# A two-layer hybrid kernel: rewritten S5 mixer (array halves, tree, straight steps) and two MoE result arrays in place of three

## The reference, cut to what matters

```python
u = grp(h); y = u * d                     # the skip with d, by channel
for di, rev in enumerate((False, True)):
    # lam_bar, b_bar from a, log_step, b
    _, h_ctx = s5_scan(u_c, lam_bar, b_bar, c_mat, h0, rev, False)    # context first
    yl_d, _ = s5_scan(u, lam_bar, b_bar, c_mat, h_ctx, rev, True)     # then the latents
    y = y + yl_d
z = gelu(y); val, gt = split(z @ glu_w + glu_b, 2)
return val * sigmoid(gt)
```

## Time and profile before

| | us |
|---|---|
| median of 3 runs | 2813.92 (2813.19 to 2816.01) |
| profiled execution, device time | 2811.32 |
| its span in the trace | 2809.6 |
| prepare | 0 to about 218 |
| mixer 0 | to 658 |
| MoE of layer 0 (route, loop, combine) | 658 to 1610 |
| S5 mixer | 1610 to 2022 |
| MoE of layer 1 | 2022 to 2809.6 |

### The profile page before, as it was taken

How to read it: one execution, slowest core, us unless ns; L and a number is a source line. 1 busy time by engine, 2 the same in 40 slices (tenths; PEclk the granted TensorE clock), 3 DMA queues, 4 the chain that set the end, 5 groups by cost and what they waited for, 6 DMA issues and landing times. The chain is left out here.

```text
span 2809.6 us, 41115 instructions
## 1 busy us (share of the span) xinstructions
PE 2204.6 (78%) x12118; PEld 1269.5 (45%) x12119; DVE 972.7 (35%) x2063; ACT 612.7 (22%) x1083; POOL 582.3 (21%) x470
## 2 busy tenths in 40 slices
PE   3877998995969999999998046099786999988882
PEld 2774544743434444444444045084343444444441
DVE  4963365933322112121121447832232111111113
ACT  2342423612112112121121031031121221211110
POOL 2750000001022222222222304000002222233332
PEclk9998999997979999999999566559897999999996
DMA  9973102005089999999997546042129999999994
GB/s 322 411 309 121 60 30 75 1 1 221 31 329 364 356 354 365 348 365 352 353 370 234 212 115 175 0 151 78 70 114 363 364 364 357 340 363 390 391 381 153
DMA packets 178229, 685.01 MB, mean 244 GB/s; under 512 B 34298, under 2 KB 37818, under 8 KB 133370
## 3 DMA queue, kind: packets, MB, share of 16 engines
q1 hardware_dynamic: 129642, 581.86, 53.5%
q0 software_dynamic: 38848, 71.14, 10.6%
q10 hardware_dynamic: 9648, 30.81, 2.7%
HBM read 628.15 MB, written 95.63 MB: 258 GB/s over the span
## 5 line engine op out<-in xcount | busy, mean ns | idle before, releaser
L1424 PE MATMUL pGUw_m<-wguw_m,xTw_m 128*128 128x512 f32 x800 | 357.8, 600 | 22.3 <-issue 21.9
L1435 PE MATMUL pGUn_m<-wgun_m,xTn_m 128*64 128x256 f32 x2816 | 323.3, 382 | 30.0 <-issue 20.5
L1435 PEld LDWEIGHTS pGUn_m<-wgun_m,xTn_m 128*64 128x64 f32 x2816 | 208.8, 137 | 175.9 <-issue 82.3
L1424 PEld LDWEIGHTS pGUw_m<-wguw_m,xTw_m 128*128 128x128 f32 x800 | 148.5, 191 | 232.8 <-issue 232.8
L1474 PE MATMUL pYn_m<-wdn_m,hidTn_m 128*64 128x512 f32 x704 | 189.9, 615 | 18.1 <-DVE hidTn_m L1379 16.3
L1453 PE MATMUL pYw_m<-wdw_m,hidTw_m 128*128 128x512 f32 x400 | 191.8, 602 | 15.5 <-DVE hidTw_m L1365 15.5
L1228 POOL DMA_INDIRECT xgw_m<-moe_h,idxw_m x58 | 60.5, 1043 | 650.4 <-PE pTw_m L1410 618.0
L1234 POOL DMA_INDIRECT xgn_m<-moe_h,idxn_m x96 | 101.4, 1056 | 250.8 <-DVE idxn_m L1355 212.4
L872 POOL MEMSET zero_r<- 128x1024 f32 x2 | 1.9, 952 | 713.2 <-POOLq L69 443.6
L1255 POOL DMA_INDIRECT moe_acc<-yn_m,idxn_m x88 | 141.4, 1607 | 27.5 <-issue 27.5
L1362 DVE TENSOR_TENSOR hidw_m<-hsilw_m,pGUw_m 128x256 f32<-128x256 f32 x50 | 21.1, 421 | 326.7 <-ACT hsilw_m L1297 326.7
(11 more groups left out here) (378 smaller groups left out, 3406.2 us busy)
## 6 DMA issues: line engine op xcount, KB each, us to landing
wgun_m<-in_exp_w_gate SPq DMA_DIRECT2D x88, 1024.0 KB, 9.9
wgun_m<-in_exp_w_up SPq DMA_DIRECT2D x88, 1024.0 KB, 15.7
wdn_m<-in_exp_w_down SPq DMA_DIRECT2D x88, 1024.0 KB, 15.8
wguw_m<-in_exp_w_gate SPq DMA_DIRECT2D x50, 1024.0 KB
wguw_m<-in_exp_w_up SPq DMA_DIRECT2D x50, 1024.0 KB
wdw_m<-in_exp_w_down SPq DMA_DIRECT2D x50, 1024.0 KB, 12.7
w_p<-in_mod_w SPq DMA_DIRECT2D x24, 2048.0 KB, 16.5
acc_c<-moe_acc SPq DMA_DIRECT2D x30, 512.0 KB, 11.3
```

The source lines that it names most:

```text
L1424: last = pe.matmul(pGU_w[:], xT_w[b % 2][:, k, :], wgu[0][b % WIDE_RING][:, :, k, :], start=(k == 0), stop=(k == KD - 1))
L1435: last = pe.matmul(pGU_n[H * side:H * side + H, b % 2], xT_n[b % 2][:, k % 4, H * (k // 4):H * (k // 4) + H], w[:, :, k, P * side:P * side ...
```

## The change

**MoE.** Array 2 is gone. Route zeroes one array on ACT's queue in place of two. All narrow adds go to array 1, and POOL waits before each that the narrow add before it has landed. Combine loads two arrays; POOL's sum is gone.

**Prepare.** The skip d is put into the table of the within-chunk matmuls: `Dd` is loaded (512 KB), multiplied by the identity on DVE, and added to the K tables by four 16x16 matmuls for each half batch. UD, the Z sum and their waits are gone from S5.

**S5 front.** X comes in four DMAs, the squares of a quarter wait only for it, and Tb's loads on POOL wait for all four. DVE squares lam four times (powers for the tree) ahead of the norm.

**Recurrence.** The 32 context chunks are folded by a tree of five levels, four operations each; the latents' 63 steps are written out one after another, with no loop.

**After it.** The Tb and from_states matmuls exchange their operands: 64 columns of U or SV are stationary, 128 columns of Tb or Wb move, and two groups lie in the two column halves of the array. The sum lies in PSUM with chunks as rows, gelu reads it there, and `turn`, 16 small matmuls by the identity for each batch, gives what the GLU needs. SP issues the first half of the GLU weights once all copies of states are done, ahead of the Wb loads of batches 6 and 7.

```diff
@@ moe_route @@
-            for acc in accs[1:]:
-                for t in range(NT):
-                    act.dma_start(acc[t * P:(t + 1) * P, :], zero[:]).then_inc(zero_out, 16)
+            for t in range(NT):
+                act.dma_start(accs[1][t * P:(t + 1) * P, :], zero[:]).then_inc(zero_out, 16)
@@ moe_loop @@
                 pool.wait_ge(N['y_done'], i + 2)
+                pool.wait_ge(yn_added[(b + 1) % 2], q * (16 * UNROLL // 2) + 16 * ((b + 1) // 2) + 16)
                 pool.sem_inc(N['pool_go'], 1)
-                pool.indirect_dma_start(acc_half[1 + b % 2], bass.IndirectOffsetOnAxis(idx[1][b][:].bitcast(U32), 0),
+                pool.indirect_dma_start(acc_half, bass.IndirectOffsetOnAxis(idx[1][b][:].bitcast(U32), 0),
@@ moe_combine @@
-        @block.gpsimd
-        def _(pool):
-            for t in range(NT):
-                pool.wait_ge(acc_in[t], 48)
-                pool.tensor_tensor(acc1[:, t, :], acc1[:, t, :], acc2[:, t, :], ALU.add).then_inc(half_sum, 1)
-
...
-                dve.wait_ge(acc_in[t], 48)
-                dve.wait_ge(half_sum, t + 1)
+                dve.wait_ge(acc_in[t], 32)
@@ prepare @@
+            sp.dma_start(Dd[:].rearrange("p g i -> p (g i)"), io['s5_d'].to_broadcast([P, SG * SI])).then_inc(S['d_in'], 16)
...
+            dve.tensor_tensor(Dd[:], Dd[:], ident[:, 0:SI].rearrange("p (o i) -> p o i", o=1).to_broadcast([P, SG, SI]),
+                              ALU.mult).then_inc(S['dd_done'], 1)
...
+                            for g in range(4):
+                                pe.matmul(pK[32 * g:32 * g + SI, 7 * SI:8 * SI], ident[:, 0:SI], Dd[:, n * GB + 4 * half + g, :],
+                                          start=False, stop=False, skip_group_check=True)
@@ s5_mixer, SP @@
-            sp.dma_start(X[:], xin.rearrange("(c t) d -> c t d", t=SL)).then_inc(S['x_in'], 16)
+            for j in range(4):
+                sp.dma_start(X[:, 2 * j:2 * j + 2, :], xin.rearrange("(c t) d -> c t d", t=SL)[:, 2 * j:2 * j + 2, :])\
+                  .then_inc(x_in[j], 16)
...
+                if b == 5:
+                    sp.wait_ge(S['t_mm'], NB)
+                    sp.wait_ge(S['sf_done'], NB)
+                    sp.wait_ge(S['sb_done'], NB)
+                    glu_half(0)
...
+            glu_half(1)
@@ s5_mixer, POOL @@
+            for j in range(4):
+                pool.wait_ge(x_in[j], 16)
...
-            pool.tensor_tensor(UD, U[:, :, 0:NCL], vcol[:, 5].rearrange("p (g o) -> p g o", o=1).to_broadcast([P, SG, NCL]),
-                               ALU.mult).then_inc(S['ud_done'], 1)
@@ s5_mixer, ACT @@
+            for b in range(3):
+                states(b)
             for b in range(NB):
...
+                gelu(b)
+                if b % 2 == 0 and b >= 2:
+                    turned(b - 1)
+                if b + 3 < NB:
+                    states(b + 3)
+            turned(NB - 1)
@@ s5_mixer, DVE @@
+            dve.wait_ge(S['l8_in'], 16)
+            for level in range(4):
+                re, im = lam[:, level, 0], lam[:, level, 1]
+                done(dve.tensor_tensor(sqr[:, 0], re, re, ALU.mult))
+                done(dve.tensor_tensor(sqr[:, 1], im, im, ALU.mult))
+                done(dve.scalar_tensor_tensor(out=lam[:, level + 1, 1], in0=re, scalar=2.0, in1=im, op0=ALU.mult, op1=ALU.mult))
+                done.wait()
+                done(dve.tensor_tensor(lam[:, level + 1, 0], sqr[:, 0], sqr[:, 1], ALU.subtract))
+                done.wait()
...
-            with dve.Fori(0, 47) as q:
...
+            for level in range(5):
+                n, step = 16 >> level, 2 << level
+                early = VH[:, step // 2 - 1:NCC:step].rearrange("p n a g -> p n (a g)")
+                late = VH[:, step - 1:NCC:step]
...
+            for q in range(STEPS):
+                prev, here = VH[:, NCC - 1 + q], VH[:, NCC + q]
...
-                dve.tensor_tensor(Z[:, b * GB:(b + 1) * GB, :], ps[:, b * 512:(b + 1) * 512].rearrange("p (g c) -> p g c", g=GB),
-                                  UD[:, b * GB:(b + 1) * GB, :], ALU.add).then_inc(S['zs_done'], 1)
@@ s5_mixer, PE @@
+            def out_of(b, h, q):
+                return ps[64 * h:64 * h + 64, b * 512 + q * P:b * 512 + (q + 1) * P]
...
+                            last = pe.matmul(out_of(b, h, q), SV[:, part, b * GB + g, :],
+                                             Wb[b % 2][:, part, g, 0:SL, :].rearrange("p k i -> p (k i)"),
+                                             start=False, stop=(part == 1), skip_group_check=True)
...
+            def turn(b):
+                pe.wait_ge(S['z_done'], b + 1)
...
+                        last = pe.matmul(ps[at, b * 512 + t * NCL:b * 512 + (t + 1) * NCL], rows[at, t], ident[at, at],
+                                         start=True, stop=True, skip_group_check=True)
+                last.then_inc(S['zT_mm'], 1)
+
+            from_states(0)
+            for b in range(1, NB):
+                from_states(b)
+                turn(b - 1)
+            turn(NB - 1)
```

More of the change, by code:

```diff
@@ L2044, in _, with states @@
                 act.activation(VH[0:64, 0:NCC, :, gs].rearrange("p c a g -> p g a c"), src[:, :, :, NCL:NCK], ACT.Copy).then_inc(S['va_done'], 1)
[L2045 to L2046 removed]
+            def states(b):
                 g = slice(b * GB, (b + 1) * GB)
@@ L2070, in _ @@
             done.wait()
-            for j in range(6):
+            for j in range(5):
                 done(dve.tensor_copy(vrep[:, j], vec[:, j:j + 1, :].to_broadcast([SG, SL, SI])))
@@ L2203, in _ @@
                 pe.wait_ge(S['sb_done'], b + 1)
-                for g in range(GB):
-                    gg = b * GB + g
+                for q in range(4):
                     for part in range(2):
-                        last = pe.matmul(ps[:, gg * NCL:(gg + 1) * NCL],
-                                         Wb[b % 2][:, part, g, 0:SL, :].rearrange("p k i -> p (k i)"),
-                                         SV[:, part, gg, :], start=False, stop=(part == 1), skip_group_check=True)
-                last.then_inc(S['o_mm'], 1)
```

170 lines of the change are left out of this document (83 added, 87 removed).

## The result

The changed kernel takes 2722.5 us (median of four runs, 2719.8 to 2723.8) against 2814.3; the ratio is 0.967, with a 95% interval of 0.966 to 0.969. That is 92 us less, where the prediction had 96. In the profiled execution the span is 2718.1 us against 2809.6.

What follows compares the result with a forecast made beforehand. The weight stream bounds the MoE loops, a serial one-engine chain the S5 mixer. Terms -31.4, -24, -11.6, -14.2, -10.0, -7.9, +1, +2 sum to -96.1: 2811.3 becomes 2715.2, or 2718 against the median; range 2698 to 2742.

Steps and rivals of the forecast that it cites:

- 63 x 1.11: Recurrence: 63 straight steps at 1.11 us each take 69.9 us, beside 19.4 for the tree; the whole term is -31.4.
- rival (4): Recurrence: straight steps still cost 1.205 us, the unrolling not doing what it says; 6 us more, 2724; chance 0.06.
- T0: The end of the recurrence, from which the tail's times are counted; GLU was forecast to start at T0 + 54.
- Rival (2): Tail: Wb 6 is not held by the GLU half, transfers overlap; GLU starts about T0 + 43, total 2707; chance 0.09.
- rival (1): Tail: PE stays at 1.2 GHz through from_states and turns; -14 in place of -24, total 2728; chance 0.15.
- Rival (5): Tail: weight loads of one half don't run beside the other half's matmuls; +20 us, total 2738; chance 0.05.
- 3.1 MB at the 425 GB/s seen elsewhere are 7.4 us: S5 front: X's transfer, with Tb waiting, takes 7.4 us, so X is there by about 1620; front's term -11.6.
- 1.4 us after X: S5 front: before the change, lam, the input of DVE's squarings, lands 1.4 us after X.
- rival (3): Layer 1's loop: narrow adds bind in part, 34 x 0.4 = 13 us, total 2731; chance 0.08.
- So the wait just fits: MoE loop: an add lands after 8.5 us, adds come every 8.75, so POOL's wait costs +1 (0 to +12).
- a sign of being wrong: MoE loop: the prediction would be wrong if POOL's wait for the add before shows idle time in each narrow item.
- Rival (6): Narrow stretch: with one array and one add in flight, adds land after 12.6 us; total 2848, slower; chance 0.03.

Runs made afterwards that it cites:

- the second trace of the change: The changed kernel run once more with no edit, beside the kernels compared with it: 2723.8 us, ratio 0.969 to the kernel before.

## Why the prediction was right

**What it said of the whole** (2718, 2698 to 2742) held, and the mechanisms were those named, but for X's rate and the price of the wait in layer 1's loop; seven of ten rows of the table lie within 4 us. That the total came within 5 us is in part luck, since errors of both signs cancelled: the S5 stages behind the front gave 12.2 us more than forecast, the start, the layer 0 stretch, the front, route 1 and layer 1's loop 16.9 less.

**Recurrence: right, its step mis-sized.** "63 x 1.11": straight steps take 1.056. The 1.11 came from a step inside the loop, which carries its own register work; the loop's turn was not all that the unrolling saves. The tree was 19.14 for 19.4, from two points of the cost per element. In a loop again the recurrence is 7.8 us longer, without the tree 13.5: both parts are shown, and rival (4), straight steps at the loop's 1.205, is out.

**Tail: right, the end taken too cold.** The copies of states ended at T0 + 23.7 for 25, Wb 6 landed at T0 + 39.8 for 42, GLU began 9.9 us after it for 12. The last is the clock: batch 6 ran at a granted clock of 0.50 (3.68 us), the turn behind it at 0.66 (1.63 us), batch 7 at 1.00 (1.97 us). That Wb 6 and 7 are held back by the GLU half was the step that mattered, and putting them first gives 7 us. Rival (2), transfers that overlap, is out by the 14.58 us; rival (1), 1.2 GHz throughout, is out: the granted clock is 0.86 on the mean from the recurrence's end to the wait.

**Weight loads of the halves.** 32 passes of 128 columns took 1.97 us, 0.062 a pass, where half of the earlier trace rows gives 0.057. From 1779.7 to 1781.7, a batch at the full clock, PE was multiplying for 1.99 of 2.00 us and loading for 1.82, so the loads lie beside matmuls; whether beside those of their own half or of the other the views do not tell. Rival (5) is out. The Trainium skill, "TensorE: Matmul & The Clock Gate", "Part 3: Packing small matmuls — row/col tiling", says that loads overlap matmuls in flight only when the row groups differ; these halves share all rows, and this trace differs from it. The same section also has loads pulled ahead when they go to the background weight buffer; the trace would fit that, but does not show where a load went.

**Front: the mechanism right, X's rate wrong.** "3.1 MB at the 425 GB/s seen elsewhere are 7.4 us" failed. X's transfer ran at 267 GB/s with the DMA busy all the time, and its last quarter landed about 1614, some 15 us after the issue. A rate seen in another stage with other rows was no bound for this one; the trace of before had 195 GB/s for the same transfer beside Tb, which was nearer. The squarings stood last, as said, and their late start came from the vectors queued behind X. The "1.4 us after X" for lam was misread: 20.4 and 19.0 us each count from their own issue, and lam's came 3.6 us later (1613.76 and 1610.12 on SP's queue), so before it landed 5 us after X; in the change it landed 0.8 us after X's last quarter. That Tb's wait is worth 6 us is shown; why X is slow with a busy DMA was not tried.

**V stage: no step of the change.** It was put at 0 and came out at -4.4. But it took 62.0 us in the run of the kernel before with the wait, which has the old S5 mixer, and 61.2 to 65.6 in the others. The clock granted to PE was 0.93 in the change's trace (above) and 0.83 in before's:

```profile
1663.70:1705.00 41.30, 36.78 (x256) 35.67 (x256) 22.15 (x31) 22.20 (x31) 0.00 (x0) 0.83 0.70 219
```

The trace of before was the slow end of a scatter of 5 to 6 us. The sum of a forecast against one trace carries that.

**Loop of layer 1: rival (3) happened.** The step that failed is "So the wait just fits": it set the landing (8.5) against the period (8.75) and put the time from a landing to the next add's start at nothing. That time is 0.8 us, and 8.5 + 0.8 is more than 8.75. So the wait ended last in nearly every item of the narrow stretch, which the prediction had named as a sign of being wrong, and the period was 9.2 us for 8.8. The first 31 gaps of the stretch took 15.4 us more than before; the last three, where the weight stream is over and the adds waited for land after 3.7 to 4.7 us, took 6.9 less. Rival (3) had put 13 us on it; 8.5 was measured, 12.5 in the second trace of the change and 11 in the kernel with the wait alone. Rival (6), landings as slow as in the mixed stretch (12.6), did not come: the median was 8.3.

**Combines and routes.** The combines came out to 0.1 us; the price of 1.22 us an operation was right, with POOL no longer at work beside DVE. The sum took 7.9 for the routes, where 4.4 and half of 7.4 make 8.1. The routes gave less than their bytes: the transposes of layer 0 wait 2.96 us less for the shared weights (30.18 for 33.14), but between the route and the first adds most of this is lost again, and from single traces it can't be told from the scatter. **Prepare:** 3.4 in this pair of traces for 2. The Dd product took 2.79 us; over all runs the route of layer 0 begins at 658 and 660 with the old prepare and at 660 to 674 with the new one, and in the two latest of them (668 and 674) DVE waits 11.6 and 13.4 us for stores of the tables, against 4.9 and 1.2 in the change's two traces. Why that varies stays open.

## What to carry to other kernels

A latency of 8.5 in a period of 8.75 is not a free wait: with one transfer in flight, the time from its landing to the next start has to fit too (0.8 us here), and a second array takes the wait off the path (8 us or more here). What is issued early for the next stage pushes back whatever is queued behind it on the same DMA queue: here two small table loads, each holding up the chain, belonged ahead of 4 MB that nobody could use yet (7 us). When an edit changes an engine's instruction count, compare stages and not totals: a loop that was not touched may run differently for its place alone.
